# Other places for the half sums of the modulation vectors

## The reference, cut to what matters

```python
shift, scale, gate = jnp.split(c_act @ w_ada[l] + b_ada[l], 3, axis=-1)
h = rms_norm(x, norm_w[l]) * (1.0 + scale[:, None, :]) + shift[:, None, :]
(gq, gk, gv, glr, gz, dq, dk, dv, da, db, dz, aq, ak, av, az) = jnp.split(h @ w_in[l], bounds, axis=-1)
...
y = jnp.concatenate([o_gla, o_gdn, o_diff], axis=-1) @ w_out[l]
x = x + gate[:, None, :] * y
```

## Time and profile before

| what | value |
| --- | --- |
| median of 3 runs | 3799.99 us (3798.98 to 3800.39) |
| profiled execution, its own time | 3798.29 us |
| its span in the trace | 3796.5 us |
| mean granted clock of TensorE | 0.942 |
| TensorE busy (matrix products) | 3391.9 us, 89% |
| VectorE busy | 1329.4 us, 35% |
| ScalarE busy | 523.3 us, 14% |
| first block, layer 0 | about 106 to 840 us of the span |
| first block, layer 1 | about 840 to 1541 us |

### The profile page before, as it was taken

The page is one execution under the profiler, slowest core; times in us unless marked ns, Lnnn a source line. Parts: engine busy times, 40 slices in busy tenths (PEclk is TensorE's granted clock), DMA queues, the critical chain, the costliest instruction groups (busy, mean ns, idle before and its releaser), DMA issues.

```text
span 3796.5 us, 57854 instructions
## 1 busy us (share of the span) xinstructions
PE 3391.9 (89%) x26734; PEld 2834.4 (75%) x26734; DVE 1329.4 (35%) x2027; ACT 523.3 (14%) x913; POOL 184.3 (5%) x249
## 2 busy tenths in 40 slices
PE   1799589999988999599997788888889999999997
PEld 1689478888876888444586677777778888888886
DVE  7543555215346521222443566665330000000001
ACT  1211001111210020300001433433110000000000
POOL 1100000000000000100000112111000000000000
PEclk6899689999998999799998899999999999999999
DMA  9732567635234534333575000000463444443442
GB/s 389 295 123 89 222 245 303 249 133 213 100 130 184 216 132 151 113 127 139 193 290 203 8 7 8 9 7 4 174 260 133 155 155 155 148 146 137 152 152 83
DMA packets 51812, 582.15 MB, mean 153 GB/s; under 512 B 7010, under 2 KB 7328, under 8 KB 8464
## 3 DMA queue, kind: packets, MB, share of 16 engines
q1 hardware_dynamic: 33664, 465.06, 32.5%
q0 software_dynamic: 17936, 113.85, 7.9%
HBM read 576.78 MB, written 2.10 MB: 152 GB/s over the span
## 4 chain that ended last, share of the span: by engine, by line
PE 79%; DVE 9%; DMA 7%; ACT 3%; issue 2%; POOL 0%; DVEq 0%; ACTq 0%; POOLq 0%
PE PS L1280 29%; PE PS L334 14%; PE PS L1359 8%; PE PS L575 6%; PE PS L331 4%; DMA ring<-in_w_vec_dram 3%; PE PS L1475 2%; PE PS L1478 2%; PE PS L1464 2%; PE PS L348 1%; DVE ring L193 1%; DMA ring<-in_w_start_dram 1%; DMA ring<-in_w_second_dram 1%; DVE ring L780 1%; ACT W L1690 1%
## 5 line engine op out<-in xcount | busy, mean ns | idle before, releaser
L1280 PE MATMUL PS<-H,ring 128*128 128x256 f32 (+2 forms) x4736 | 1156.1, 407 | 42.9 <-ACT H L1621 30.9
L1280 PEld LDWEIGHTS PS<-H,ring 128*128 128x128 f32 (+1 forms) x4736 | 902.5, 191 | 296.4 <-issue 151.5
L334 PE MATMUL PS<-H,ring 128*128 128x256 f32 x3072 | 698.2, 387 | 73.2 <-DMA ring<-in_w_first_dram 69.2
L334 PEld LDWEIGHTS PS<-H,ring 128*128 128x128 f32 x3072 | 589.7, 194 | 163.2 <-DMA ring<-in_w_first_dram 69.7
L1359 PE MATMUL PS<-Pj,ring 128*128 128x256 f32 x1408 | 304.2, 379 | 1.2 <-DVE small L1928 1.2
L1359 PEld LDWEIGHTS PS<-Pj,ring 128*128 128x128 f32 x1408 | 267.4, 190 | 37.9 <-issue 1.6
L780 DVE SCALAR_TENSOR_TENSOR ring<-ring,H 128x2048 f32<-128x2048 f32 x96 | 219.1, 2289 | 161.6 <-DMA ring<-in_w_vec_dram 153.5
L575 PE MATMUL PS<-H,ring 128*128 128x256 f32 x1024 | 222.5, 379 | 2.9 <-DVE H L1031 2.9
L1922 DVE TENSOR_TENSOR Pj<-W,PS 128x512 f32 (+1 forms) x22 | 15.1, 687 | 597.3 <-PE PS L1280 597.3
L575 PEld LDWEIGHTS PS<-H,ring 128*128 128x128 f32 x1024 | 194.4, 190 | 30.0 <-issue 3.6
L331 PE MATMUL PS<-ring,H 128*128 128x256 f32 x768 | 172.0, 387 | 0.0
(11 more groups left out here) (401 smaller groups left out, 3112.4 us busy)
## 6 DMA issues: line engine op xcount, KB each, us to landing
ring<-in_w_second_dram SPq DMA_DIRECT2D x105, 2048.0 KB, 7.8
ring<-in_w_first_dram SPq DMA_DIRECT2D x76, 2048.0 KB, 8.0
ring<-in_w_vec_dram POOLq DMA_DIRECT2D x96, 1024.0 KB, 6.7
ring<-in_w_second_dram SPq DMA_DIRECT2D x32, 1408.0 KB, 6.0
ring<-in_w_start_dram SPq DMA_DIRECT2D x16, 2048.0 KB, 10.1
Pj<-in_x_dram SPq DMA_DIRECT2D x1, 2048.0 KB, 10.6
H<-in_cvecs_dram POOLq DMA_DIRECT2D x2, 1024.0 KB, 13.8
H<-in_cvecs_dram POOLq DMA_DIRECT2D x1, 2048.0 KB, 10.0
```

What stands on the lines that cost most here:

```text
L334: mm = pe.matmul(PS[:, t % 2, half * T:(half + 1) * T], ring[:, t % 2, k, half * P:(half + 1) * P], hT[:, k, :], start=(k == 0), stop=(k = ...
L1280: mm = pe.matmul(PS[0:cols, bank(q, half), 0:width], ring[:, q % RING].rearrange("p k n -> p (k n)")[:, k * 2 * cols + half * cols:k * 2 * ...
```

## The change

Counts of halves are moved between the places. Per layer the total stays 64 and 32. In numbers, as (layer 0, layer 1): behind the modulated input (6, 6), behind the GLA decay (6, 6), behind the convolved tiles 4 to 9 in layer 0 alone 3, 3, 2, 2, 2, 0, ahead of the first head norm none, ahead of the query norm (4, 3), behind the query rotation (10, 7), behind the key rotation (14, 10), behind the softmax unchanged. The narrow weights of layer 1 come behind the issue of half 20.

```diff
@@ -285,7 +285,7 @@
             for i in range(VEC0[l], VEC0[l + 1]):
                 pool.wait_ge(vec_done.sem, vec_done.start + i - 1)
                 half_loaded[i % 2].inc(pool.dma_start(half_slot(i % 2), A["w_vec"][i]), 16)
-                if i == 3 and l < NL - 1:
+                if i == 20 and l < NL - 1:
                     pool.wait_ge(S("narrow").sem, S("narrow").at(l, 1))
                     narrow_weights(l + 1)
             if l < NL - 1:
@@ -816,6 +816,8 @@
             while 32 * (freed[0] + 1) <= BEFORE[name]:
                 if 4 <= freed[0] < 10:
                     conv(freed[0])
+                    if l == 0:
+                        vectors((3, 3, 2, 2, 2, 0)[freed[0] - 4])
                 freed[0] += 1
 
         do(v.tensor_tensor(lamp, vcol(l, V_LAM, V_END)[:, 0:4:2], vcol(l, V_LAM, V_END)[:, 1:4:2], ALU.mult), S("lam_prod"))
@@ -829,7 +831,7 @@
         need(S("h_ready"), KC)
         if l:
             v.wait_ge(S("c_next").sem, 1)
-        vectors((6, 4)[l], slots(W, 0, 8))
+        vectors(6, slots(W, 0, 8))
 
         need(S("lam_exp"), 1)
         do(stt(lamv[:, 2:3], lamv[:, 1:2], -1.0, lamv[:, 0:1], ALU.mult, ALU.add))
@@ -961,7 +963,6 @@
         need(S("dl_ks"), 1)
         do(v.tensor_tensor(rhs1.rearrange("p a (b d) -> p (a b) d", d=P), vtok[:, :, P:T], PS[:, 6, :].rearrange("p (h c) -> p h c", h=4), ALU.subtract), S("dl_r1"))
         need(S("dl_out"), 1)
-        vectors((8, 5)[l], slots(W, 16, 24))
         gates()
 
         need(S("o_ssq"), 1)
@@ -971,7 +972,7 @@
         need(S("o_nb"), 1)
         do(stt(wide(o_gla), wide(o_gla), vcol(l, V_GLAN, V_GLAN + 1), PS[:, 4:6, :]))
         do(stt(wide(o_gdn), wide(o_gdn), vcol(l, V_GDNN, V_GDNN + 1), PS[:, 6:8, :]), S("o_normed"))
-        vectors((8, 5)[l], slots(W, 16, 24))
+        vectors((4, 3)[l], slots(W, 16, 24))
 
         lo, hi = slice(0, 64), slice(64, 128)
         for r in range(2):
@@ -990,7 +991,7 @@
             do(v.tensor_tensor(x_, x_, cosT.unsqueeze(1).to_broadcast([P, 8, T]), ALU.mult))
             settle()
             do(v.tensor_tensor(x_, x_, turned_, ALU.add), S("at_rope") if r else None)
-            vectors((12, 7)[l], slots(W, 16, 24))
+            vectors(((10, 14), (7, 10))[l][r], slots(W, 16, 24))
         settle()
         for n in range(8):
             need(S("at_scores"), n + 1)
```

## The result

The changed kernel takes **3734.1 us** (median of 4 runs, 3729.5 to 3742.3), the kernel before beside it 3800.2 (3799.0 to 3802.1, 4 runs). The ratio is 0.983, with a 95% interval of 0.981 to 0.985. The forecast was 3735 in a range of 3714 to 3764. The span of the profiled execution fell from 3796.5 to 3733.1 us, by 63.4, where the sum of the prediction had 65.3.

A forecast was written before the change was run, and what follows sets the result against it. The prediction took TensorE idling behind VectorE's groups of halves, which wait for loads, and the lowered clock after it as the bound. Gains less costs summed to 65.3 us, giving a 3734.7 us median, range 3714 to 3764.

The forecast's parts named there:

- Rival (e): Nothing changes, because halves are bound by their loads wherever they stand: 3800 us, chance 0.02.
- First head norms: No halves ahead of them removes TensorE's waits of 22.07 and 16.65 us and clock loss: gains 27.9 and 21.5.
- Query and key norm of layer 0: Halves cut 8 to 4 and 12 to 10, so VectorE comes sooner: gains 16.9 and 7.8 us, clock loss staying.
- Scores of layer 0: Halves ahead of the scores raised 12 to 14, delaying the first maximum slightly: cost 1 us.
- Behind the convolved tiles: Layer 0: the third half delays the GLA states, 3.2 us wait plus 1.8 clock; the rest covered by idle time.
- Layer 1, the decay: Halves 4 to 6 without cover; sixth loads late: 8.7 us wait plus 4 for the clock, cost 12.7.
- Layer 1, key norm: Seven halves before and after, so the 1.59 us wait stays: no gain.
- Narrow weights: Next layer's narrow weights moved from fourth to twenty-first half on POOL's queue: nothing, between -1 and +1 us.
- (b): The two new stalls, at layer 0's GLA states and layer 1's decay, don't come: 17.7 us more gain, 3717, chance 0.14.
- (a): Denser products bring tile loads closer, slowing late halves by 1.5 us each: 24 us back, 3759, chance 0.21.
- (c): Slower than before: halves behind convolutions and four in layer 1 on the path, 92 us lost: 3808, chance 0.03.
- (d): Loads wait for VectorE's operation to end, each new late half issued up to 2.3 us later: 3739, chance 0.04.

The follow-up runs named there:

- noload: Changed kernel with only the first two halves loaded, later sums over what lies in the ring, modulation not the right one: 3695.4 us.
- l0only: The change in layer 0 alone, layer 1 with the counts of the kernel before: 3753.8 us, ratio 0.989.
- again: The changed kernel run once more as it is: 3735.5 us (5 runs), its profiled execution 3742.5.
- tail2: Changed kernel with 4 halves instead of 6 behind layer 1's GLA decay, the other two in that layer's tail: 3720.7 us.
- key8: Changed kernel with 8 halves ahead of layer 0's key norm and 16 ahead of its scores, for 10 and 14: 3741.1 us.
- best: Changed kernel with halves moved to cover its remaining waits (convolved tiles 2, 5, 2, 2, 3; key norms 8 and 6; four in layer 1's tail): 3706.2 us.
- narrow3: Changed kernel with the narrow weights of layer 1 back behind the issue of half 3: 3736.4 us.
- small: Changed kernel with each half's load cut to 64 of 2048 columns (32 KB), sums full width, modulation not the right one: 3709.2 us.

## Why the prediction was right, and where its steps were not

**What bounds the kernel.** Right. In the first block the time moved with TensorE's idle time behind VectorE's groups and with the clock behind it; noload shows how little is left of both when no half is waited for. Rival (e), no change, is out by 66 us.

**First head norms (27.9 and 21.5).** Right in kind; measured 26.2 and 19.8. Both are some 1.7 us short, nearly all of it in the filler behind `over_rows`: in layer 0 it took 8.65 us for 32 records, not the 7.2 that I had worked out from 28 at full clock, and in layer 1, where I had counted 1.4 us back, it gave nothing back. Even without a gap these products did not run at full clock: 404.2 to 412.6 us has a granted clock of 0.82.

**Query and key norm of layer 0 (16.9 and 7.8).** Each was off, the sum was not: 24.7 forecast, 25.6 measured. I left 1 us of wait and the whole clock loss at the query norm; TensorE came working and lost neither (23.7). But the end of the key norm's wait is set by VectorE's ten halves, which start from the query norm. By the starts of `over_rows` both steps hold: the query norm's moved by 39.5 us (461.99 to 422.51) where the terms up to it give 27.9 + 16.9 - 5 = 39.8, and the key norm's by 48.1 (541.10 to 492.98) for 47.6. What TensorE's full clock gained between the two, it spent waiting: it came 5.8 us earlier in the changed kernel's trace than the same products at the old clock would have, and the wait was 5.0 longer than forecast. The step that failed is the booking of the clock's return as lost at the one place and of the wait as shorter at the other. With it failed one sign of the forecast: it had 2 to 8 us of idle time before the third `over_rows`, and 9.29 came. The group itself was also slower when a tile's load went ahead of its third half: from the first issue to the tenth half 47.7 us (440.41 to 488.08), against 44.9 in l0only (442.15 to 487.08).

**Scores of layer 0 (-1).** The wait is 0 or about 4.4 us by execution (none in the first trace, 4.42 in again, 4.32 in tail2), some 6.4 with the clock behind it, and so part of the spread of the changed kernel's runs. The 1 that was forecast is neither. key8 shows where cover ends: with two halves more the wait was 8.2.

**Behind the convolved tiles (-5).** Right: 2.42 us of wait, and the output products at a lower clock. That the rest was free is shown by the 12.09 us that were left, and by best, which puts five halves behind the second tile at no wait of TensorE.

**Layer 1, the decay (-12.7).** The wait was right (8.7 forecast, 9.59 measured), and so was its reason, the sixth half that can only be issued when the fourth is done. The clock behind it was undersized: 4 forecast, 6.5 measured, 4.8 of it in the first 80 us. tail2 gives the term back: 13.4 us in the medians, 16.7 in layer 1 of its trace.

**Layer 1, key norm (0).** 2.0 came that were not forecast: the wait went from 1.59 to 1.29 us, and the same 16 records from 6.46 to 5.23.

**Narrow weights (0).** Right, by narrow3.

**The sum.** 65.3 forecast, 63.4 measured. That it is so close is partly luck. The first head norms (1.7 each) and the decay (3.4) fell short by 6.8 together, and the GLA states (0.9), the scores (1), the query and key norm of layer 0 (0.9 together) and those of layer 1 (0.6 and 2.0) gave 5.4 back. The trace of again ends 7.6 us later with the same program.

**The rivals.** (b), the stalls that don't come, failed at both places. (a), halves slowed by denser products, did not come as priced, 24 us in all; what is seen of its mechanism is the 2.7 us in the key norm's group. (c) did not come. (d), loads held up until VectorE's operation ends, would have added up to 2.3 us to each late half. The Trainium skill ("SBUF — State Buffer", section "SBUF: two separate sides") has it for VectorE's two-port modes. No row shows that: in small the sum that began at 445.07 runs for 2.29 us, to 447.36, and the load issued beside it at 445.45 was used at 447.52. It cannot have started after the sum and landed 0.16 us later. Whether this sum runs in such a mode no run here shows, so this says nothing on operations that do.

## What to carry over

When side work with its own loads is spread over an engine that others wait for, count for each place how many pieces are already there (here two) and how much slack follows; only the pieces beyond them cost, and those cost a load, not their work. Look for places where the engine idles anyway: here the tail of layer 1 and the stretch behind the norm took halves for nothing, and, with the waits that are left, brought 35 us on top of the change's 66. A term ahead of a point that loads set is not a gain by itself: check what the next wait is measured from before adding up. And a term of a few us is to be read where the edit acts: at the end of the program the second block's own spread of 14 us covers it.

## What the runs showed of the hardware that I had not expected

- A transfer of 32 KB on POOL's queue takes 2.07 us from issue to use alone, and 7.93 when a 2 MB load on SP's queue was issued 0.14 us before it. For 1 MB halves the same difference is 5.1 to 5.5 against 11.1 to 11.3.
- A difference of 2 us in the order of two issues changes a wait by 5 to 6 us, and goes itself with TensorE's clock. The nine traces agree on that; no run tried it by itself. With a wait of 0 or 4.4 us at the seventh score this is part of the spread of the changed kernel (3729.5 to 3743.0 over 9 runs). The kernel before spreads as far: 3787.5 to 3802.7 in the runs beside best.
- The second block, the same in every version, took 2180.9 to 2194.8 us in 14 traces, without a cause that they show.
- TensorE's products with 8 partitions of input took 3.71 us (16 records) when nothing was idle before them in most traces, but 3.9 to 5.1 in some, and mostly 5.1 to 6.5 behind waits of 0.9 to 1.7 us (1119.28 and 1186.78 above, 5.99 and 5.23). One wait of that length, in tail2, left them at 3.71:

```profile
1109.44 3.71 PE L348 MATMUL PS<-W,con 8*128 8x256 f32 x16 [1.28 <-DVE W L984]
```

What lowers the clock in the executions without a gap, and what spared this one, stays open.
